# A decoder trunk on one core: the moving operands of the feed-forward products and the attention stage's regions laid at differing bytes modulo 64

## The chip, the core and the metric

The kernel runs on one core of one Trainium2 chip. The metric is device time in microseconds of that core, from the first to the last instruction of one launch with what lies around it. Lower is better. TensorE is called PE here, VectorE DVE, ScalarE ACT, GpSimd POOL and SyncE SP; PEld is the loading of PE's stationary operand, which the profile shows on a row of its own.

## What is computed

Two layers of a hybrid decoder over 512 tokens of 1024 channels, in float32, then a final norm:

```python
for l in range(2):
    h = rms_norm(x)                       # (512, 1024)
    proj = h @ w_in                       # 6656 columns: q, k, v, rotary q, k, v, gate g_r, merge gates
    y_a = stick_breaking(q, k, v) @ sb_w_out          # 8 heads of 64
    y_b = (group_norm(retention(q_r, k_r, v_r)) * silu(g_r)) @ ret_w_out   # 4 heads
    x = x + (g_a * y_a + g_b * y_b) @ w_o
    a, b = split(rms_norm(x) @ w_up)      # 2 * 2816 columns
    x = x + (silu(causal_conv3(a)) * b) @ w_down
return rms_norm(x)
```

## The kernel before

**Products in three passes.** Every large product is done with each float32 operand split into a high part (rounded to the format fp32r, which PE takes in one pass) and a low part (the rest). For one tile of 128 x 128 of the stationary operand and 256 or 512 columns of the moving operand, PE does three matmuls: high times high, high times low, low times high. `three` and `three_open` write them out. Each matmul loads its own stationary tile, so one weight load belongs to one matmul. ACT makes the high parts (copies into fp32r) and DVE the low parts (a subtraction).

**Who is moving and who is stationary.** In the projections from `w_in`, in the products with `sb_w_out`, `ret_w_out` and `w_o`, and in the first two pairs of up-projection tiles, the weight slab (`w_hi`, `w_lo`) is stationary and the token operand moves, 512 columns at a time: `u_hi`/`u_lo` (normed input), `osb` (attention output), `or_hi`/`or_lo` (retention output), `m_hi`/`m_lo` (merged branches). For the value columns it is the other way round: `u_hi`/`u_lo` stationary, the slab moving.

**Seven products.** The rest of the up-projection (9 rounds of two pairs a layer) is done by a Strassen-like scheme: the tokens and the channels are halved, seven combinations of the quarters are made once per layer (`comb_hi[k]`, `comb_lo[k]`, k = 0 to 6, each 4 tiles of 256 columns), and `product(n, k, ...)` multiplies combination k with a combination of the weight quarters. One product is 24 matmuls: 2 column tiles, 4 contraction tiles, 3 passes, each with `comb_hi[k]` or `comb_lo[k]` moving, 256 columns. Two layers of 9 rounds of 7 products are 3024 matmuls of 256 columns. The down-projection uses the same scheme with 7 products of 21 chunks in all: the gated activation is cut in chunks (`chunk_hi[n % 3]`, `chunk_lo[n % 3]`), of which the first two of three lie in `comb_hi[3]`, `comb_lo[3]` and `comb_hi[4]`, `comb_lo[4]` and the third in `chunk_hi2`, `chunk_lo2`. In layer 0 (`down_unit`) the chunk moves, 256 columns: 924 matmuls, of which 336, 336 and 252 read chunk 0, 1 and 2. In layer 1 (`token_unit`) the chunk is stationary and the weights move, 512 columns: 462 matmuls, 168, 168 and 126.

**Where the tiles lie.** SBUF tensors are placed by hand: `sb(name, shape, dt, where)` places a tile at byte `where` of each partition. The first tiles (`xs`, `u_hi`, `u_lo`, `w_hi`, `w_raw`, with `far_*` over them) come one after another. From `M` on lie the regions of the attention stage (`QK`, `VS`, `RQK`, `VR_`, `SG_`, `G_`, `TMP`), which the feed-forward stage uses anew: `g_raw`, `comb_hi[k]` at `s_hi_at[k]`, `comb_lo[k]` at `s_lo_at[k]`, and so on. All regions are whole multiples of 1024 bytes from `M`, and

```python
assert M % 64 == u_hi_at % 64 == w_hi_at % 64 == ring_at % 64
```

so that both operands of every large matmul start at the same byte modulo 64: byte 32. All but a few start at byte 32 modulo 128 too. The few lie behind the two buffers `ca` (8 * (S + 8) = 4160 bytes, which is 65 times 64): `comb_lo[5]`, `comb_hi[6]`, `comb_lo[6]`, `chunk_hi2` and `chunk_lo2` start at byte 96 modulo 128. A tile within an operand begins at a multiple of 512 bytes from the operand's start, so it keeps these remainders.

**Order.** Each engine has its own instruction list, written out by hand and tied by semaphores; PE's list is unrolled, 9106 matmuls.

Of the kernel before, what the change touches and what calls it, by code (L numbers as in the profile page):

```python
# [22 lines left out]
F32 = mybir.dt.float32  # L23
# [3 lines left out]
P = 128  # L27
S = 512
# [126 lines left out]
def trunk(nc, xt, wts, wdn, par, consts, rope, decay, last, out):  # L155
    with ExitStack() as ctx:
# [5 lines left out]
        def sb(name, shape, dt, where=None):  # L162
            n = 1
            for s in shape[1:]:
                n *= s
            size = n * {BF16: 2, mybir.dt.uint8: 1}.get(dt, 4)
            if where is None:
                where = at[0]
                at[0] += (size + 31) // 32 * 32
            return nc.alloc_sbuf_tensor_at(name, shape, dt, offset=where)  # L170

        K = 1024
        x_at = at[0] + 4 * KT
        xs = sb("xs", [P, KT + KT * S], F32)
        x = xs[:, KT:].rearrange("p (k s) -> p k s", k=KT)
        u_hi_at = at[0]
        u_hi = sb("u_hi", [P, KT, S], F32R)
        far_raw = sb("far_raw", [P, 4, SLAB], F32, u_hi_at)
        far_lo = sb("far_lo", [P, 4, SLAB], F32R, u_hi_at)
        u_lo_at = at[0]  # L180
# [20 lines left out]

        M = at[0] + 32
        assert M % 64 == u_hi_at % 64 == w_hi_at % 64 == ring_at % 64
        QK, VS, RQK, VR_, SG_, G_ = M, M + 16 * K, M + 32 * K, M + 48 * K, M + 64 * K, M + 80 * K
        TMP = M + 112 * K
        q2 = sb("q2", [P, SB_HEADS, S], F32R, QK)
        k2 = sb("k2", [P, SB_HEADS, S], F32R, G_)
        q_lo = [sb(f"q_lo{p}", [P, 2, S], F32R, (SG_ + 12 * K, TMP + 5 * K, G_ + 22 * K, G_ + 26 * K)[p])
                for p in range(SB_PAIRS)]
# [25 lines left out]

        att = sb("att", [P, ECOLS], F32, TMP)
        att_lo = sb("att_lo", [P, S], F32R, TMP)
        att_hi = sb("att_hi", [P, S], F32R, TMP + 2 * K)
        st_last = sb("st_last", [P, 256], F32R, TMP + 4 * K)
        beta = sb("beta", [P, ECOLS], F32, G_ + 16 * K)  # L240
        sp_hi = sb("sp_hi", [P, ECOLS], F32R, G_ + 16 * K)
        sp_lo = sb("sp_lo", [P, ECOLS], F32R, TMP)
        ynorm = sb("ynorm", [P, TT, 256], F32, TMP + 5 * K)
        g_raw = sb("g_raw", [P, FT, S], F32, M)
        first_raw = sb("first_raw", [P, 4, SLAB], F32, M + 28 * K)
        XYU = M + 88 * K + 8 * (S + 8) + 8 * K
        copy_x = sb("copy_x", [P, 2, S // 2], F32, XYU)
        copy_y = sb("copy_y", [P, 2, S // 2], F32, XYU + 2 * K)
        copy_u = sb("copy_u", [P, 2, S // 2], F32, XYU + 4 * K)
        late2 = sb("late2", [P, 4, S // 2], F32, XYU)  # L250
        PAST = XYU + 6 * K
        s_hi_at = [M + (44 + 8 * k) * K for k in range(6)] + [PAST + 4 * K]
        s_lo_at = [M + (48 + 8 * k) * K for k in range(5)] + [PAST, PAST + 8 * K]
        comb = [sb(f"comb{k}", [P, 4, S // 2], F32, s_lo_at[k]) for k in range(7)]
        comb_lo = [sb(f"comb_lo{k}", [P, 4, S // 2], F32R, s_lo_at[k]) for k in range(7)]
        comb_hi = [sb(f"comb_hi{k}", [P, 4, S // 2], F32R, s_hi_at[k]) for k in range(7)]
        t_raw = sb("t_raw", [P, PIECES, SLAB], F32, M + 44 * K)
        chunk_hi = [comb_hi[3], comb_hi[4], sb("chunk_hi2", [P, 4, S // 2], F32R, PAST)]
        chunk_lo = [comb_lo[3], comb_lo[4], sb("chunk_lo2", [P, 4, S // 2], F32R, XYU)]
        s_raw = [sb(f"s_raw{i}", [P, 4, S // 2], F32, M + at_k) for i, at_k in enumerate((84 * K, 88 * K, 92 * K + K // 2))]  # L260
        ca = sb("ca", [P, 2, S + 8], F32, M + 88 * K)
        cb_at = M + 88 * K + 8 * (S + 8)
        cb = sb("cb", [P, 2, S], F32, cb_at)
        cc = sb("cc", [P, 2, S], F32, cb_at + 4 * K)
        lastg = sb("lastg", [P, D], F32, cb_at + 4 * K)
# [1958 lines left out]
```

## Time and profile before

| | |
|---|---|
| median of 3 runs | 1582.34 us (1582.21 to 1583.85) |
| the profiled execution | 1581.26 us |
| its span, first to last instruction | 1579.5 us |
| PE busy | 1566.5 us, 99% |
| weight loads (PEld) busy | 1383.8 us, 88% |
| DVE busy | 1171.5 us, 74% |
| ACT busy | 769.3 us, 49% |
| POOL busy | 250.6 us, 16% |
| mean granted TensorE clock | 0.999 |

Matmuls are pipelined, and the length that the profile gives for one overlaps that of the next. What a matmul costs in a row of them is the distance from its start to the next one's start; it is called the pitch here. It is read from the timeline, as the time between two starts divided by the number of matmuls between them.

### The profile page before, as it was taken

To read this page: it belongs to the slowest core of one execution; us is meant where nothing else is said; L and a number is where in the kernel's file an instruction comes from. 1 tells how busy PE (TensorE), PEld (TensorE's weight loads), DVE (VectorE), ACT (ScalarE), POOL (GpSimd) and SP (SyncE) were. 2 spreads that over 40 slices of the span, in tenths; PEclk is the share of its full clock that TensorE was granted. 3 is DMA by queue.
4 is the path that set the end of the run, shared out by engine and by line. 5 is a ranking of instruction groups with operands and counts; after the bars stand their busy time and mean duration, and the time that the engine had idled before them with its cause. 6 is when DMAs were issued, how large, how long until landed. Compare 5 with 4: busy or idle time off the path is not lost. (4 is left out here: it accounts for less than half of the span.)

```text
span 1579.5 us, 22764 instructions
## 1 busy us (share of the span) xinstructions
PE 1566.5 (99%) x9106; PEld 1383.8 (88%) x9106; DVE 1171.5 (74%) x1295; ACT 769.3 (49%) x982; POOL 250.6 (16%) x270
## 2 busy tenths in 40 slices
PE   9999999999999999999999999999999999999998
PEld 7888888888888999999988888888888899999776
DVE  7257876786679877796972678658756898777877
ACT  5344334542355555664533533355332565556646
POOL 4000000000230222241240000000002212223310
PEclk9999999999999999999999999999999999999999
DMA  5332222222227888899223322222222388888991
GB/s 195 99 122 75 79 81 93 80 68 93 94 94 240 239 233 237 264 239 260 97 96 104 114 75 78 81 94 70 78 94 93 100 251 237 237 237 277 229 271 64
DMA packets 66628, 231.41 MB, mean 147 GB/s; under 512 B 7392, under 2 KB 7904, under 8 KB 66528
## 3 DMA queue, kind: packets, MB, share of 16 engines
q1 hardware_dynamic: 52272, 182.93, 33.4%
q0 software_dynamic: 12096, 41.95, 14.7%
q10 hardware_dynamic: 2160, 5.12, 1.1%
q8 instruction: 72, 1.18, 0.3%
q14 instruction: 28, 0.23, 0.0%
HBM read 225.78 MB, written 2.10 MB: 144 GB/s over the span
## 5 line engine op out<-in xcount | busy, mean ns | idle before, releaser
L1748 PE MATMUL ps<-u_hi,w_hi 128*128 128x512 f32 x768 | 301.3, 392 | 0.0
L1749 PE MATMUL ps<-u_lo,w_hi 128*128 128x512 f32 x768 | 299.3, 390 | 0.0
L1750 PE MATMUL ps<-u_hi,w_lo 128*128 128x512 f32 x768 | 299.1, 390 | 0.0
L1186 DVE TENSOR_TENSOR w_lo<-w_raw,w_hi 128x1024 fp32r<-128x1024 f32 x158 | 208.6, 1333 | 68.3 <-ACT w_hi L752 67.9
L752 ACT ACTIVATE w_hi<-w_raw 128x1024 fp32r<-128x1024 f32 x158 | 164.3, 1052 | 76.6 <-DMA w_raw<-wts 70.2
L1754 PE MATMUL ps<-comb_hi,far_hi 128*128 128x256 f32 x688 | 194.5, 283 | 0.0
L1755 PE MATMUL ps<-comb_lo,far_hi 128*128 128x256 f32 x688 | 194.1, 282 | 0.0
L1756 PE MATMUL ps<-comb_hi,far_lo 128*128 128x256 f32 x624 | 175.7, 282 | 0.0
L1750 PEld LDWEIGHTS ps<-u_hi,w_lo 128*128 128x128 f32 x768 | 144.2, 188 | 30.4
L1748 PEld LDWEIGHTS ps<-u_hi,w_hi 128*128 128x128 f32 x768 | 144.4, 188 | 28.4
L1749 PEld LDWEIGHTS ps<-u_lo,w_hi 128*128 128x128 f32 x768 | 144.4, 188 | 28.3
L1754 PE MATMUL ps<-comb_hi,w_hi 128*128 128x256 f32 x544 | 154.2, 283 | 0.4 <-DVE comb_lo L1415 0.3
L1756 PE MATMUL ps<-comb_hi,w_lo 128*128 128x256 f32 x544 | 153.8, 283 | 0.0
L1755 PE MATMUL ps<-comb_lo,w_hi 128*128 128x256 f32 x544 | 153.2, 282 | 0.0
L1754 PEld LDWEIGHTS ps<-comb_hi,far_hi 128*128 128x128 f32 x688 | 131.4, 191 | 0.8 <-issue 0.5
L1755 PEld LDWEIGHTS ps<-comb_lo,far_hi 128*128 128x128 f32 x688 | 131.5, 191 | 0.0
L1756 PEld LDWEIGHTS ps<-comb_hi,far_lo 128*128 128x128 f32 x624 | 118.8, 190 | 0.0
L1754 PEld LDWEIGHTS ps<-comb_hi,w_hi 128*128 128x128 f32 x544 | 103.5, 190 | 2.0 <-DVE w_lo L1349 0.6
L1756 PEld LDWEIGHTS ps<-comb_hi,w_lo 128*128 128x128 f32 x544 | 104.2, 192 | 0.0
L1755 PEld LDWEIGHTS ps<-comb_lo,w_hi 128*128 128x128 f32 x544 | 103.6, 190 | 0.0
L713 POOL TENSOR_TENSOR g_raw<-cc,cb 128x512 f32<-128x512 f32 x36 | 73.5, 2059 | 186.4 <-ACT cc L834 186.4
L1349 DVE TENSOR_TENSOR far_lo<-far_raw,far_hi 128x1024 fp32r<-128x1024 f32 x48 | 58.8, 1224 | 48.4 <-ACT far_hi L821 47.2
(325 smaller groups left out, 3402.6 us busy)
## 6 DMA issues: line engine op xcount, KB each, us to landing
w_raw<-wts SPq DMA_DIRECT2D x212, 512.0 KB, 3.5
far_raw<-wts SPq DMA_DIRECT2D x56, 512.0 KB, 3.6
t_raw<-wdn POOLq DMA_DIRECT2D x30, 512.0 KB, 9.8
w_raw<-wdn SPq DMA_DIRECT2D x24, 512.0 KB, 7.0
w_raw<-wts POOLq DMA_DIRECT2D x18, 512.0 KB, 10.3
far_raw<-wts POOLq DMA_DIRECT2D x16, 512.0 KB, 7.0
far_raw<-wdn SPq DMA_DIRECT2D x16, 512.0 KB, 8.3
t_raw<-wdn SPq DMA_DIRECT2D x10, 512.0 KB, 5.9
```

Of the source, the lines that this page charges most:

```text
L713: nc.gpsimd.tensor_tensor(g_raw[:, f, :], cc[:, h, :], cb[:, h, :], ALU.mult).then_inc(s_gf, 1)
L752: nc.scalar.activation(w_hi[:, s, :], w_raw[:, s, :], ACT.Copy).then_inc(s_hi, 1)
L1186: nc.vector.tensor_tensor(w_lo[:, s, :], w_raw[:, s, :], w_hi[:, s, :].bitcast(F32), ALU.subtract).then_inc(s_lo, 1)
L1349: nc.vector.tensor_tensor(part_lo(l, n, k), part_raw(l, n, k), part_hi(l, k).bitcast(F32), ALU.subtract).then_inc(s_elo, 1)
L1748: nc.tensor.matmul(dst, a_hi, b_hi, start=start, stop=False)
L1749: nc.tensor.matmul(dst, a_hi, b_lo, start=False, stop=False)
L1750: return nc.tensor.matmul(dst, a_lo, b_hi, start=False, stop=stop)
L1754: nc.tensor.matmul(dst, a_hi, b_hi, start=start, stop=False, skip_group_check=True)
L1755: nc.tensor.matmul(dst, a_hi, b_lo, start=False, stop=False, skip_group_check=True)
L1756: return nc.tensor.matmul(dst, a_lo, b_hi, start=False, stop=stop, skip_group_check=True)
```

## The change

No instruction is added, removed or moved, and none changes its shape: each engine has the same instructions in the same order, and only addresses differ. `sb` learns to place a tile at a byte that is no multiple of 32: it allocates a slightly wider tile at the multiple of 32 below and returns the part of it that begins at the wanted byte. Then

- the regions of the attention stage are displaced by 8 bytes (`QK`, `VS`), 16 bytes (`RQK`, `VR_`, `SG_`) and 48 bytes (`G_`), and `TMP` by 64;
- the moving operands of the seven products are displaced by `APART[k]` = 8, 16, 24, 40, 48, 56, 68 bytes, the high and the low part of one k alike;
- what lies behind them is pushed on by 64 bytes to make room, so that `chunk_hi2` and `chunk_lo2` come to byte 32 modulo 128.

The slabs and parts of the weights (`w_*`, `far_*`), `u_hi`, `u_lo`, `g_raw`, `t_raw` and `first_raw` stay where they were.

```diff
-            return nc.alloc_sbuf_tensor_at(name, shape, dt, offset=where)
+            if where % 32 == 0:
+                return nc.alloc_sbuf_tensor_at(name, shape, dt, offset=where)
+            apart = where % 32 // 4
+            tile = nc.alloc_sbuf_tensor_at(name, [shape[0], apart + n], dt, offset=where - 4 * apart)[:, apart:apart + n]
...
-        QK, VS, RQK, VR_, SG_, G_ = M, M + 16 * K, M + 32 * K, M + 48 * K, M + 64 * K, M + 80 * K
-        TMP = M + 112 * K
+        QK, VS, RQK, VR_, SG_, G_ = M + 8, M + 16 * K + 8, M + 32 * K + 16, M + 48 * K + 16, M + 64 * K + 16, M + 80 * K + 48
+        TMP = M + 112 * K + 64
...
-        XYU = M + 88 * K + 8 * (S + 8) + 8 * K
+        XYU = M + 88 * K + 8 * (S + 8) + 8 * K + 64
...
-        s_hi_at = [M + (44 + 8 * k) * K for k in range(6)] + [PAST + 4 * K]
-        s_lo_at = [M + (48 + 8 * k) * K for k in range(5)] + [PAST, PAST + 8 * K]
+        APART = (8, 16, 24, 40, 48, 56, 68)
+        s_hi_at = [M + (44 + 8 * k) * K + APART[k] for k in range(6)] + [PAST + 4 * K + 64 + APART[6]]
+        s_lo_at = [M + (48 + 8 * k) * K + APART[k] for k in range(5)] + [PAST + APART[5], PAST + 8 * K + 64 + APART[6]]
...
-        ca = sb("ca", [P, 2, S + 8], F32, M + 88 * K)
-        cb_at = M + 88 * K + 8 * (S + 8)
+        ca = sb("ca", [P, 2, S + 8], F32, M + 88 * K + 64)
+        cb_at = M + 88 * K + 8 * (S + 8) + 64
```

How far the two operands of a matmul lie apart modulo 128, before and after, with the number of matmuls:

| matmuls | columns | before | after |
|---|---|---|---|
| products 0 to 4 of the up-projection | 2160 of 256 | 0 | 8, 16, 24, 40, 48 |
| product 5 | 432 of 256 | 0 (high part), 64 (low) | 56 |
| product 6 | 432 of 256 | 64 | 4 |
| down-projection, layer 0, chunks 0 and 1 | 672 of 256 | 0 | 40, 48 |
| the same, chunk 2 | 252 of 256 | 64 | 0 |
| `osb`; `or`; `m` with weight slabs | 192; 384; 384 of 512 | 0 | 8; 16; 48 |
| down-projection, layer 1, chunks 0 and 1 | 336 of 512 | 0 | 88, 80 |
| the same, chunk 2 | 126 of 512 | 64 | 0 |
| `u_hi`, `u_lo` with weight slabs | 2904 of 512 | 0 | 0 |

The remaining matmuls, some 830, belong to the attention heads and the retention and are mostly narrower.

## Rows read from the trace of the kernel before

**Rows 1.** The page: span, busy time and, in 40 slices, the granted clock.

```profile
span 1579.5 us, 22764 instructions
PE 1566.5 (99%) x9106; PEld 1383.8 (88%) x9106; DVE 1171.5 (74%) x1295; ACT 769.3 (49%) x982; POOL 250.6 (16%) x270
...
PEclk9999999999999999999999999999999999999999
```

**Rows 2.** PE's waits: line, waited for: us in total, times, longest.

```profile
PE ps L2076 <- ACT xt_early L885: 2.9, 1, 2.9
PE ps L1754 <- DVE chunk_lo L1415: 2.2, 3, 1.2
```

**Rows 3.** Groups by shape: moving and stationary operand | busy us, mean ns | idle.

```profile
L1748 PE MATMUL ps<-u_hi,w_hi 128*128 128x512 f32 x768 | 301.3, 392 | 0.0
...
L1754 PE MATMUL ps<-comb_hi,far_hi 128*128 128x256 f32 x688 | 194.5, 283 | 0.0
...
L1748 PE MATMUL ps<-or_hi,w_hi 128*128 128x512 f32 x128 | 50.0, 390 | 0.0
L1748 PE MATMUL ps<-m_hi,w_hi 128*128 128x512 f32 x128 | 49.8, 389 | 0.0
```

**Rows 4.** Timeline of PE, products 2 and 3: start us; 49 rows, first and last.

```profile
581.65 0.28 PE L1754 MATMUL ps<-comb_hi,far_hi 128*128 128x256 f32 x1
...
587.41 0.28 PE L1754 MATMUL ps<-comb_hi,far_hi 128*128 128x256 f32 x1
```

**Rows 5.** Timeline of PE, products 5 and 6: 49 rows, first and last.

```profile
590.29 0.28 PE L1754 MATMUL ps<-comb_hi,far_hi 128*128 128x256 f32 x1
...
595.94 0.28 PE L1754 MATMUL ps<-comb_hi,w_hi 128*128 128x256 f32 x1
```

**Rows 6.** Timeline of PE, product 6 of the first round: 21 rows.

```profile
513.06 0.28 PE L1756 MATMUL ps<-comb_hi,far_lo 128*128 128x256 f32 x1
...
515.33 0.28 PE L1755 MATMUL ps<-comb_lo,w_hi 128*128 128x256 f32 x1
```

**Rows 7.** Timeline of PE, output projection, 512 columns: 25 rows.

```profile
430.17 0.39 PE L1748 MATMUL ps<-m_hi,w_hi 128*128 128x512 f32 x1
...
435.61 0.39 PE L1748 MATMUL ps<-m_hi,w_hi 128*128 128x512 f32 x1
```

**Rows 8.** Timeline of PE, token stage, chunk 2, 512 columns: 19 rows.

```profile
1492.21 0.40 PE L1754 MATMUL ps<-w_hi,chunk_hi 128*128 128x512 f32 x1
...
1496.40 0.39 PE L1754 MATMUL ps<-far_hi,comb_hi 128*128 128x512 f32 x1
```

**Rows 9.** Timeline of PE after the scores of one head.

```profile
125.21 0.40 PE L1748 MATMUL ps<-u_hi,w_hi 128*128 128x512 f32 x1
125.45 0.40 PE L1749 MATMUL ps<-u_lo,w_hi 128*128 128x512 f32 x1
125.68 0.39 PE L1750 MATMUL ps<-u_hi,w_lo 128*128 128x512 f32 x1
125.91 0.40 PE L1748 MATMUL ps<-u_hi,w_hi 128*128 128x512 f32 x1
...
126.38 0.39 PE L1750 MATMUL ps<-u_hi,w_lo 128*128 128x512 f32 x1
126.60 0.39 PE L1748 MATMUL ps<-u_hi,w_hi 128*128 128x512 f32 x1
```

**Rows 10.** VectorE's two convolution lines: duration ns min/median/max.

```profile
L1386 DVE SCALAR_TENSOR_TENSOR cc<-ca,pars,cc x44: 736/744/752, 477.4 to 1465.1; 128x512 f32<-128x512 f32 x44
...
L1389 DVE SCALAR_TENSOR_TENSOR cc<-ca,pars,cc x44: 750/752/754, 478.2 to 1465.9; 128x512 f32<-128x512 f32 x44
```

**Rows 11.** Stretches: busy us of PE, PEld, DVE, ACT, POOL; clock, DMA share.

```profile
600.00:640.00 40.00, 40.00 (x338) 40.00 (x337) 31.84 (x33) 23.31 (x30) 11.76 (x8) 1.00 0.83 235
680.00:720.00 40.00, 40.00 (x337) 40.00 (x337) 37.94 (x35) 20.92 (x23) 16.35 (x16) 1.00 1.05 228
```

**Rows 12.** The DMA that copies the queries: count, KB each, us to landing.

```profile
q<-q ACTq DMA_DIRECT2D x8, 256.0 KB, 3.7
```

More of the change, by code:

```diff
@@ L169, in sb @@
                 at[0] += (size + 31) // 32 * 32
-            return nc.alloc_sbuf_tensor_at(name, shape, dt, offset=where)
+            if where % 32 == 0:
+                return nc.alloc_sbuf_tensor_at(name, shape, dt, offset=where)
+            apart = where % 32 // 4
+            tile = nc.alloc_sbuf_tensor_at(name, [shape[0], apart + n], dt, offset=where - 4 * apart)[:, apart:apart + n]
+            if len(shape) == 2:
+                return tile
+            letters = "abcde"[:len(shape) - 1]
+            return tile.rearrange(f"p ({' '.join(letters)}) -> p {' '.join(letters)}", **dict(zip(letters[1:], shape[2:])))
         K = 1024
@@ L259, in trunk @@
         chunk_lo = [comb_lo[3], comb_lo[4], sb("chunk_lo2", [P, 4, S // 2], F32R, XYU)]
-        s_raw = [sb(f"s_raw{i}", [P, 4, S // 2], F32, M + at_k) for i, at_k in enumerate((84 * K, 88 * K, 92 * K + K // 2))]
-        ca = sb("ca", [P, 2, S + 8], F32, M + 88 * K)
-        cb_at = M + 88 * K + 8 * (S + 8)
+        s_raw = [sb(f"s_raw{i}", [P, 4, S // 2], F32, M + at_k) for i, at_k in enumerate((84 * K + 64, 88 * K + 64, 92 * K + K // 2 + 64))]
+        ca = sb("ca", [P, 2, S + 8], F32, M + 88 * K + 64)
+        cb_at = M + 88 * K + 8 * (S + 8) + 64
         cb = sb("cb", [P, 2, S], F32, cb_at)
```

## The prediction

> **What bounds the kernel now.** I read the page first: PE is busy for 1566.5 of 1579.5 us and its clock is at the full level, 2.4 GHz, in all 40 slices [rows 1]. Then what PE waits for: the longest entries are 2.9 and 2.2 us in all [rows 2]. So no transfer and no other engine sets the time; the sum of the distances between PE's matmuls does. The change touches no instruction, only the addresses that matmuls read. It can matter only through the pitch of a matmul, and the question is whether pitch depends on address.
>
> The grouped rows do not answer that, since their mean length overlaps the next matmul's: 283 ns for 256 columns, 389 to 392 ns for 512 [rows 3]. The timeline does. In products 2 and 3 of a late round, 48 matmuls of 256 columns start within 587.41 - 581.65 = 5.76 us: 120.0 ns each [rows 4]. The next two but one, products 5 and 6, take 595.94 - 590.29 = 5.65 us for 48: 117.7 ns each [rows 5]. Clock, shape and engine are the same. What differs is the place: `comb_lo[5]`, `comb_hi[6]` and `comb_lo[6]` lie 64 bytes off modulo 128 against the weights, while in products 2 and 3 both operands lie alike. Product 6 of the first round, entered after a wait and not from a running stream, does 20 matmuls in 515.33 - 513.06 = 2.27 us: 113.5 ns each [rows 6]. Streaming 256 columns at 2.4 GHz takes 106.7 ns, so the part over it is 13.3, 11.0 or 6.8 ns.
>
> With 512 columns the sign is the other way. Operands that lie alike: 24 in 435.61 - 430.17 = 5.44 us, 226.7 ns [rows 7], again 13.3 ns over the 213.3 ns of streaming. With chunk 2, 64 bytes off: 18 in 1496.40 - 1492.21 = 4.19 us, 232.8 ns [rows 8]. And even where operands lie alike the pitch has a memory: after a head's scores five matmuls take 126.38 - 125.21 = 1.17 us, 234 ns each, before the stream settles; the next one takes 0.22 us [rows 9]. So weight load and moving stream meet in some pattern that settles into a steady pitch, and the pattern knows the operands' relative place. The trace shows it at two relative places only, 0 and 64; the change moves to 4, 8, 16, 24, 40, 48, 56, 80 and 88, which no row shows.
>
> **A rule against the trace.** The Trainium skill, "SBUF — State Buffer", section "Who interferes with whom", gives PE two independent read ports, one for the moving operand and one for the weight load, and says that PE never waits on anyone. By that rule the relative place would not matter and the sum of this change would be nothing, 1582 us. The 120.0, 117.7 and 113.5 ns above, for one and the same shape, do not fit it, so the sum below goes by the rows.
>
> **The change, part by part.**
>
> *Products 0 to 4 and chunks 0 and 1 of layer 0's down-projection*: 2160 + 672 = 2832 matmuls of 256 columns leave the place where the pitch is 120.0 ns. Bounds: 113.5 ns [rows 6], which gives -6.5 ns each, -18.4 us; and 120.0 ns as now, nothing. Above 120.0 I know no steady row of this shape; for an upper bound I take the 6.1 ns by which the displaced 512-column row is dearer [rows 7, 8]: +17.3 us. I take 117.0 ns, near the 117.7 ns of the common displaced case with a little weight on 113.5: -3.0 x 2832 = -8.5 us.
>
> *Products 5 and 6*: 864 matmuls at 117.7 ns now. Bounds 113.5 (-3.6 us) and 120.0 (+2.0 us). At 117.0: -0.6 us.
>
> *Chunk 2 of layer 0's down-projection*: 252 matmuls come to lie alike, 117.7 to 120.0 ns: +0.6 us.
>
> *Output projection, retention output, attention output, and chunks 0 and 1 of layer 1*: 384 + 384 + 192 + 336 = 1296 matmuls of 512 columns leave the place where the pitch is 226.7 ns. Bounds: 232.8 ns [rows 8], +7.9 us; and, downwards, the same 6.5 ns that the 256-column rows have been seen to lose, -8.4 us. The nearest row is the one at 232.8, but it is one place out of many; I take half of its price, +3.05 ns: +4.0 us.
>
> *Chunk 2 of layer 1*: 126 matmuls from 232.8 to 226.7 ns, -0.8 us, and the irregular matmuls behind each of its seven stretches are fewer; -1.0 us together.
>
> *Attention and retention*: some 830 mostly narrower matmuls; at 3 ns either way 2.5 us, taken as nothing and kept for the range.
>
> *The unchanged 2904 matmuls of 512 columns* stay at 226.7 ns. Where they follow a displaced stretch they may need a few matmuls to settle, as in [rows 9], where five cost 5 x (234 - 226.7) = 37 ns. Some 40 such places would be 1.5 us, and most are there already; nothing.
>
> *DVE, ACT, POOL and the DMAs* get operands at bytes that are multiples of 4. Two convolution lines read `ca` one element past its start and at its start: 744 and 752 ns [rows 10]; a displaced read costs DVE nothing. The copy of the queries lands in 3.7 us [rows 12]; its target is now at another byte, and if it took twice as long, eight copies would cost at most 30 us in all, but PE has no wait for them among its longest [rows 2] and only a part of that could show. I put it at nothing. The engines behind PE have room in the rounds of seven products, DVE 31.84 and DMA 0.83 of 40 us [rows 11], so a 3% faster PE is still fed. In layer 0's down-projection DVE is busy for 37.94 us of 40 and the DMA share is 1.05, so there a gain much above 5% would turn into a wait for `chunk_lo`; at 2.5% it doesn't.
>
> Sum: -8.5 - 0.6 + 0.6 + 4.0 - 1.0 = -5.5 us. The profiled execution took 1581.26 us, 1.1 us under the median; so 1575.8 us on its scale and 1576.8 on the median's: **1577 us**.
>
> **The rivals.**
>
> *Strong gain (0.18).* The new places let the stream settle at 113.5 ns as in [rows 6]: 2832 x -6.5 = -18.4, 864 x -4.2 = -3.6, and the 512-column part between -4 and +4: 1556 to 1564, about 1560 us. For it: that pitch exists and is steady over 20 matmuls. Against it: in late rounds product 6 lies at the same place and does not reach it [rows 5].
>
> *Slower (0.34).* What decides is that lying exactly alike is the steady case, and each other place keeps the stream irregular. Then the 1296 wide matmuls go to 232.8 ns, +7.9 us, while the narrow ones stay at 120.0, and products 5 and 6 lose their 2.3 ns, +2.0; with +0.6 and -1.0 that is +9.5 us: 1592 us. It turns slower as soon as the wide loss, up to 7.9 us, outweighs the narrow gain: with the wide ones at 232.8 the narrow pitch must come under 117.4 ns to break even (products 5 and 6 included). The narrow pitch itself could rise, to 1600 and more. For it: [rows 8]; against it: [rows 5, 6], where displaced narrow matmuls are cheaper.
> Beside this rival stands a rule: the Trainium skill, "SBUF — State Buffer", section "Specifications (TRN2)", speaks of cachelines of 16 bytes and of a penalty for each crossing into a new one. An operand that starts 8 or 4 bytes into such a line touches one line more, in products 0, 2, 3, 5, 6 and `osb`, not in 1 and 4, `or` and `m`. No row of before has such an operand.
>
> *Nothing happens (0.19).* Only the 64-byte step counts, and smaller displacements are rounded away: products 0 to 4 stay at 120.0 ns, the wide ones at 226.7, and what is left, chunk 2 and products 5 and 6, is +0.6 - 1.0 + 2.0 = +1.6 us: 1584 us. For it: everything in the trace is in steps of 64; against it: nothing I can show.
>
> **How the numbers follow.** The forecast case, a small net gain, has 0.29, and ranges from 1568 to 1581. With the strong gain, the slower case and no effect, 0.18 + 0.34 + 0.19, that is all. The low end takes in the centre of the strong gain, 1560; the high end reaches past the slower case's 1592 to 1595. A measurement of this kernel tells 0.2%, 3.2 us, from no change. Faster by more than that: the strong gain and nearly all of the forecast case, 0.45. Within it: 0.21. Slower: 0.34.
>
> **What would show it.** In the timeline of the changed kernel: products 0 to 4 at about 117 ns a matmul instead of 120.0, and not all alike, since each k has its own displacement; `or`, `m` and `osb` at about 230 ns; `u` stretches at 226.7 as before; chunk 2 at 120.0 (256 columns) and 226.7 (512). PE's waits should stay under 15 us in all. The prediction is wrong if the products stay at 120.0 to the nanosecond (no effect of small steps), if any k stands above 120 (the slower case or worse), or if the wide matmuls drop below 226.7, which no row of before has.

## The result: slower by 0.4%

Before took 1582.98 us (1582.21 to 1583.85, 4 runs), the changed kernel 1588.32 us (1587.86 to 1590.89, 4 runs): a ratio of 1.0039, 95% interval 1.0027 to 1.0052. The forecast was 1577 us, faster, with a range from 1560 to 1595; the time lies on the other side of no change, within the range.

The page of the kernel after, with the lines that answer to [rows 1]:

```profile
span 1586.9 us, 22764 instructions
...
PE 1574.0 (99%) x9106; PEld 1384.2 (87%) x9106; DVE 1171.6 (74%) x1295; ACT 769.6 (48%) x982; POOL 250.4 (16%) x270
...
PEclk9999999999999999999999999999999999999999
```

PE is still busy for 99% of the span, at the full clock in all 40 slices, so the 7.4 us more of this span (1586.9 - 1579.5) are PE's own. PE's waits (line, waited for: us in total, times, longest), for [rows 2]:

```profile
PE ps L1762 <- DVE chunk_lo L1423: 2.9, 3, 1.4
...
PE ps L2084 <- ACT xt_early L893: 1.1, 1, 1.1
PE ps L1762 <- DVE cb L1379: 1.0, 1, 1.0
```

With the new one, for `cb`, they come to 5.0 us, against 5.1 in [rows 2]: no longer than before. The groups by shape, for [rows 3]:

```profile
L1756 PE MATMUL ps<-or_hi,w_hi 128*128 128x512 f32 x128 | 50.6, 395 | 0.0
...
L1756 PE MATMUL ps<-m_hi,w_hi 128*128 128x512 f32 x128 | 50.4, 394 | 0.0
```

The mean of the displaced wide matmuls rose from 389 or 390 ns to 394 or 395. That mean overlaps with the next matmul, so what a matmul costs has to be read from the starts. The timeline of PE after, a few starts (in us, then the modelled length):

```profile
364.54 0.47 PE L1756 MATMUL ps<-or_hi,w_hi 128*128 128x512 f32 x1
...
409.10 0.39 PE L1756 MATMUL ps<-m_hi,w_hi 128*128 128x512 f32 x1
...
453.26 0.39 PE L1756 MATMUL ps<-u_hi,w_hi 128*128 128x512 f32 x1
...
581.67 0.28 PE L1762 MATMUL ps<-comb_hi,w_hi 128*128 128x256 f32 x1
...
584.47 0.28 PE L1762 MATMUL ps<-comb_hi,far_hi 128*128 128x256 f32 x1
...
587.35 0.28 PE L1762 MATMUL ps<-comb_hi,far_hi 128*128 128x256 f32 x1
...
595.93 0.28 PE L1762 MATMUL ps<-comb_hi,w_hi 128*128 128x256 f32 x1
...
598.87 0.28 PE L1762 MATMUL ps<-comb_hi,w_hi 128*128 128x256 f32 x1
...
1194.26 0.40 PE L1756 MATMUL ps<-m_hi,w_hi 128*128 128x512 f32 x1
...
1239.06 0.39 PE L1756 MATMUL ps<-u_hi,w_hi 128*128 128x512 f32 x1
```

From 364.54 to 409.10 lie the 192 matmuls of `or` in layer 0 (16 bytes further from their weights than before): 232.1 ns each. From 409.10 to 453.26 lie the 192 of `m` (48 bytes): 230.0 ns; from 1194.26 to 1239.06 those of `m` in layer 1, at the same addresses: 233.3 ns. So one place can have more than one steady pitch. Before, `or` took 227.2 ns read in the same way and `m` the 226.7 ns of [rows 7]. Product 1 (16 bytes) is the 24 matmuls from 581.67 to 584.47, 116.7 ns; product 2 (24 bytes) follows to 587.35, 120.0 ns; product 6 (4 bytes, 595.93 to 598.87) takes 122.5 ns, where [rows 5] had 117.7. So some narrow products gained, some did not, one lost, and every wide one lost.

Read that way over all rounds (means of the distances of a product, first round and waits left out), the pitch stands so:

| product | 0 | 1 | 2 | 3 | 4 | 5 | 6 |
|---|---|---|---|---|---|---|---|
| before, ns | 119.4 | 120.0 | 120.0 | 120.0 | 120.0 | 118.0 | 117.6 |
| after: distance of its high tile | 8 | 16 | 24 | 40 | 48 | 56 | 4 |
| after, ns | 118.0 | 116.6 | 120.1 | 119.6 | 118.3 | 119.2 | 122.5 |

### The profile page after: what moved, and what is told of

Read it like the earlier page. It is cut to its first block, busy times and chain, and to the rows that moved or that the text cites. A ratio compares the mean times of both kernels' runs of the same rounds, so it can differ in the third digit from the quotient of the medians.

```text
span 1586.9 us, 22764 instructions
## 1 busy us (share of the span) xinstructions
PE 1574.0 (99%) x9106; PEld 1384.2 (87%) x9106; DVE 1171.6 (74%) x1295; ACT 769.6 (48%) x982; POOL 250.4 (16%) x270
## 3 DMA queue, kind: packets, MB, share of 16 engines
q10 hardware_dynamic: 2160, 5.12, 1.1%
## 4 chain that ended last, share of the span: by engine, by line
PE 96%; DMA 3%; DVE 0%; issue 0%; ACT 0%; POOL 0%; DVEq 0%; POOLq 0%; ACTq 0%
PE ps L1756 19%; PE ps L1758 19%; PE ps L1757 18%; PE ps L1762 12%; PE ps L1764 12%; PE ps L1763 12%; DMA far_raw<-wdn 1%; PE ps L1885 1%; PE ps L1874 1%; DMA w_raw<-wdn 1%; PE ps L1852 1%; PE ps L1856 1%; PE ps L2009 0%; PE ps L1896 0%; PE ps L1822 0%
## 5 line engine op out<-in xcount | busy, mean ns | idle before, releaser
L1764 PEld LDWEIGHTS ps<-comb_hi,far_lo 128*128 128x128 f32 x624 | 117.8, 189 | 0.0
```

What stands on the lines that cost most here:

```text
L1764: return nc.tensor.matmul(dst, a_lo, b_hi, start=False, stop=stop, skip_group_check=True)
```

## The experiments

"Distance" is the place of the token operand less the place of the weight operand, modulo 128 bytes unless another number is named. Ratios are to the kernel before, run on the same chip alongside; they are the ones on record, and differ by up to 0.05% from the quotient of the two medians. The pitches, waits and stage times of a kernel come from one profiled execution. The first four kernels ran together (before: 1581.47 us, 29 runs).

**e1_regions: only the attention regions are displaced.** The regions and `TMP` lie as in the change; the products' tiles and what lies behind them are back where they were before. In part:

```diff
-        APART = (8, 16, 24, 40, 48, 56, 68)
+        APART = (0, 0, 0, 0, 0, 0, 0)
```

> The kernel before, with only the attention stage's regions displaced as in the change (8, 8, 16, 16, 16, 48 bytes); the products' tiles stay. Theory P (the pitch of a matmul follows from the relative place of its two operands, matmul by matmul, so the parts of the change add up): the 960 matmuls of 512 columns that move osb, or and m go from about 227 to about 232 ns, 960 x 5 ns = +4.8 us, the rest unchanged: about +5 us, ratio 1.003. Rival Q (the loss comes from the products that are off the 16-byte grid, and the wide matmuls matter only through them): under +1 us.

It took 1587.02 us (5 executions), ratio 1.0040 (1.0027 to 1.0053): the whole loss. Theory P, with 1.003, holds; rival Q does not. Its timeline of PE around `m` in layer 0:

```profile
408.51 0.40 PE L1756 MATMUL ps<-m_hi,w_hi 128*128 128x512 f32 x1
...
453.31 0.39 PE L1756 MATMUL ps<-u_hi,w_hi 128*128 128x512 f32 x1
```

192 matmuls in 44.80 us are 233.3 ns each, against 226.7 before. All `or`, `m` and `osb` of both layers came to 231.6, 233.3 and 232.7 ns; here `m` was at 233.3 in both layers.

**e2_products: only the tiles of the seven products are displaced.** The edit is the other half, with `APART` kept:

```diff
-        QK, VS, RQK, VR_, SG_, G_ = M + 8, M + 16 * K + 8, M + 32 * K + 16, M + 48 * K + 16, M + 64 * K + 16, M + 80 * K + 48
+        QK, VS, RQK, VR_, SG_, G_ = M, M + 16 * K, M + 32 * K, M + 48 * K, M + 64 * K, M + 80 * K
```

> The kernel before, with only the tiles of the seven products displaced (8, 16, 24, 40, 48, 56, 68) and what lies behind them pushed on; the attention regions stay. Theory P, from the changed kernel's pitches by product (118.0, 116.6, 120.1, 119.6, 118.3, 119.2, 122.5 ns against 119.4, 120, 120, 120, 120, 118.0, 117.6) and +6.5 ns for 336 wide matmuls of layer 1's down-projection: -0.6 -1.5 +0.1 -0.3 -1.3 +0.5 +2.1 +0.3 +2.2 = about +1.5 us, ratio 1.001. Rival Q: nearly all of the change's +5.3 us.

1581.5 us, ratio 0.9997 (0.9988 to 1.0006), without a twelfth execution that took 5547.74 us: no difference, where theory P had 1.001. Each product showed the pitch of the table above. The narrow matmuls earned nothing that can be measured (the 1.7 us that the wide ones of layer 1's down-projection lose are in this time as well). The two halves, +0.40% and -0.03%, add up to the change's +0.39% as well as such intervals can tell.

**e4_base32: every tile 32 bytes further.** Operands keep their relative places, and all bytes modulo 64 change from 32 to 0:

```diff
-        at = [(nc.sbuf_base + 31) // 32 * 32]
+        at = [(nc.sbuf_base + 31) // 32 * 32 + 32]
```

> The kernel before, with every tile pushed on by 32 bytes: all operands keep their relative places, but start at byte 0 modulo 64 instead of 32. Theory P (the relative place): within 0.1% of before, pitches 120.0, 117.7 and 226.7 ns to the nanosecond. Rival S (the absolute place: a start inside a block of 64 bytes costs part of a block more): the 13.3 ns over streaming shrink, by up to 6.7 ns each for some 8000 matmuls, tens of us faster.

1581.47 us, ratio 0.9998 (0.9989 to 1.0007). Its products 1 to 4 ran at 120.0 ns, product 6 at 117.6 and `m` at 226.7, each as before. A common step of 32 bytes changes nothing, so rival S is out; what counts is where the two operands lie against each other.

**e3_all16: the best distance for all products, 0 for the wide ones.** All seven products and layer 0's chunks at 16 bytes, regions and layer 1's chunks at 0; the chunks get tiles of their own in each layer. In part:

```diff
-        APART = (8, 16, 24, 40, 48, 56, 68)
+        APART = (16, 16, 16, 16, 16, 16, 16)
...
-        chunk_hi = [comb_hi[3], comb_hi[4], sb("chunk_hi2", [P, 4, S // 2], F32R, PAST)]
+        CHUNK = (16, 0)
+        chunk_hi = [[sb(f"chunk_hi{l}_{c}", [P, 4, S // 2], F32R, w + CHUNK[l]) for c, w in enumerate((M + 68 * K, M + 76 * K, PAST))]
+                    for l in range(DEPTH)]
...
```

> The kernel before, with all seven products' moving operands displaced by 16 bytes, and layer 0's chunks too; layer 1's chunks (stationary there) stay at 0, and so do the attention regions. Theory P: every one of them at the 116.6 ns that product 1 has at 16 bytes: 2160 x -3.4 - 432 x 1.4 - 432 x 1.0 - 672 x 3.4 - 252 x 1.1 = about -11 us, ratio 0.993. Rival R (product 1 is cheap because of the product ahead of it, not because of its 16 bytes): the products settle near 120 and the time is within 2 us of before.

1579.72 us, ratio 0.9988 (0.9978 to 0.9998): 1.8 us instead of 11. One round of its timeline, products 0 to 4:

```profile
598.66 0.28 PE L1765 MATMUL ps<-comb_hi,w_hi 128*128 128x256 f32 x1
...
609.54 0.28 PE L1765 MATMUL ps<-comb_hi,far_hi 128*128 128x256 f32 x1
```

These are 96 matmuls in 10.88 us, 113.3 ns each, the lowest pitch seen; in most rounds it was 116.7, in a few 118.7, and in one round 120.0. So the step on which I had counted, a lower pitch, was there, and the gain still was not. The sum of all the distances between narrow matmuls that are under 135 ns fell from 467.1 to 457.8 us (3916 and 3909 of 3948). What stood against it were PE's waits:

```profile
PE ps L1765 <- DVE chunk_lo L1426: 4.3, 4, 1.7
PE ps L2087 <- ACT xt_early L896: 2.6, 1, 2.6
PE ps L1765 <- DVE cb L1382: 1.9, 4, 0.7
PE ps L1765 <- DVE w_lo L1415: 1.7, 1, 1.7
```

chunk_lo and xt_early went from 5.1 us to 6.9, and two new ones, for `cb` and `w_lo`, add 3.6. Summed over the whole feed-forward stages, what the distances hold beyond a regular pitch rose from 9.9 to 16.9 us. By their means (119.3 and 117.1 ns) the pace gained 8.6 us; less 7.0 us that leaves 1.6, beside the 1.0 by which the two spans differ.

The next three ran together (before: 1583.2 us, 23 runs).

**e7_down0: all products at 16, both down-projections at 0.** It asks whether PE's pace counts in the down-projection of layer 0.

```diff
-        CHUNK = (16, 0)
+        CHUNK = (0, 0)
```

> As the kernel with all at 16 bytes, but the first layer's down-projection reads its chunks at distance 0 again, so that some 910 matmuls go back from 117 to 120 ns, 2.5 to 3 us of TensorE's own work more. Theory W (the end of the first layer's down-projection is bound by the tiles that VectorE and the DMA queues make ready, so that a faster TensorE only waits longer): the time is that of the kernel with all at 16 within 0.05%, ratio to before 0.999, and the waits of more than 1 us near 732, 746 and 751 us shrink by the 2.5 to 3 us. Rival R (TensorE's pace binds there): 3 us slower than the kernel with all at 16, ratio to before 1.001.

1579.21 us, ratio 0.9977 (0.9967 to 0.9987). Its stretches (busy us and count of PE, PEld, DVE, ACT, POOL; clock, DMA share, GB/s), then PE's waits within them, first for e3_all16:

```profile
725.00:765.00 40.00, 35.66 (x296) 34.77 (x295) 31.00 (x29) 19.81 (x22) 3.50 (x4) 1.00 0.73 205
...
PE ps L1765 <- DVE chunk_lo L1426: 2.6, 3, 1.7
PE ps L1765 <- DVE w_lo L1415: 1.7, 1, 1.7
```

and for e7_down0:

```profile
725.00:765.00 40.00, 38.89 (x326) 38.72 (x325) 35.32 (x33) 23.54 (x27) 3.49 (x4) 1.00 0.74 213
...
PE ps L1765 <- DVE chunk_lo L1426: 1.1, 1, 1.1
```

With the faster pitch PE was busy for only 35.66 of the 40 us and issued 296 matmuls in them; with the slower one 326. The 924 matmuls of that projection went from 117.2 to 119.5 ns, 2.1 us more, and still layer 0's products and down-projection together took 291.0 us instead of 293.5. In these two profiles PE's faster pace in this stage is worth nothing, as theory W has it. By how much the stage comes out shorter they do not tell: the down-projection of layer 0 took 113.8 us in e3_all16 and 111.8 here, but 113.4 when this same program ran again (e9_repeat), and 112.3 with the faster pitch in e6_all16b. The total was forecast to stay at e3_all16's 0.9988; the two intervals overlap.

**e6_all16b: products 5 and 6 at 16 modulo 256 too.** As e3_all16, and:

```diff
-        s_lo_at = [M + (48 + 8 * k) * K + APART[k] for k in range(5)] + [PAST + APART[5], PAST + 8 * K + APART[6]]
+        s_lo_at = [M + (48 + 8 * k) * K + LOW[k] for k in range(5)] + [PAST + LOW[5], PAST + 8 * K + LOW[6]]
```

with `LOW[5]`, `LOW[6]` and `APART[6]` at 144.

> As the kernel with all at 16 bytes, but products 5 and 6 lie 16 bytes from their weights modulo 256 and not only modulo 128. Theory P256 (the pattern repeats with 256 bytes or more): both fall from 117.8 and 118.6 ns to 116.7, 864 matmuls in 1.3 us less. Rival P128 (it repeats with 128): they stay. In the time, if TensorE's own pace still binds in the rounds, 1 us less than the kernel with all at 16, ratio to before 0.998; if the waits for the copies of product 6 take the gain up, 0.999 as there.

1578.68 us, ratio 0.9980 (0.9966 to 0.9994). Neither theory's numbers came out, since the common level had changed. Product 4 was at 118.7 ns in 15 of 18 rounds, at 116.7 in two and at 113.3 in one, at the same addresses as in e3_all16, where it was at 116.7 in 13 rounds. Products 5 and 6 fell in with it: where the round stood at 118.7 they did too, and in the two rounds at 116.7 product 5 was at 116.7 and 116.8. In e3_all16, at 16 modulo 128 but with its low tile at 144 modulo 256, product 5 stood at 117.8 beside neighbours at 116.7. So 16 and 144 modulo 256 are different places, and distances modulo 128 do not say it all. Its products 1 to 3 in a round, 72 matmuls in 8.54 us (118.6 ns):

```profile
540.68 0.28 PE L1766 MATMUL ps<-comb_hi,w_hi 128*128 128x256 f32 x1
...
549.22 0.28 PE L1766 MATMUL ps<-comb_hi,far_hi 128*128 128x256 f32 x1
```

**e5_scan: other distances.** Products 0 to 6 at 4, 12, 20, 32, 36, 64 and 96 bytes (the low tile of 5 at 192 and both of 6 at 224 modulo 256), `osb` and `or` at 32, `m` at 64.

```diff
-        APART = (8, 16, 24, 40, 48, 56, 68)
+        APART = (4, 12, 20, 32, 36, 64, 96)
```

> A map rather than a bet on the time. The operands of the products lie 4, 12, 20, 32, 36 and 64 (192 for its low tile) bytes from those of the weights, product 6 at 224 modulo 256; osb and or at 32, m at 64. Theory P (only the distance 0 lets 512 columns run at 226.7 ns; every other distance costs them 2% to 3%): or, osb and m all come out at 231 to 234 ns, the four stages of or and m together 3 to 5 us longer than before, and the time 2 to 6 us above the kernel before. Rival G (the pattern repeats with 64 bytes or 32): m at 64 stays at 226.7 ns, and with 32 or and osb too, so that the time is within 0.1% of before or lower by what the products gain. For the products, if a displacement of 4 inside 16 bytes is what made product 6 slow (122.5 ns), products 0, 2 and 4 (4, 20 and 36) are at 121 to 123 ns; if it was something of that place alone, they are at 116 to 120.

1590.99 us, ratio 1.0046 (1.0029 to 1.0063). Its timeline: `m` between the first two starts, then products 5, 6, 0, 1 and 2 in turn:

```profile
409.68 0.39 PE L1756 MATMUL ps<-m_hi,w_hi 128*128 128x512 f32 x1
...
453.63 0.39 PE L1756 MATMUL ps<-u_hi,w_hi 128*128 128x512 f32 x1
...
593.97 0.28 PE L1762 MATMUL ps<-comb_hi,far_hi 128*128 128x256 f32 x1
...
596.80 0.28 PE L1762 MATMUL ps<-comb_hi,w_hi 128*128 128x256 f32 x1
...
599.64 0.28 PE L1762 MATMUL ps<-comb_hi,w_hi 128*128 128x256 f32 x1
...
602.60 0.28 PE L1762 MATMUL ps<-comb_hi,w_hi 128*128 128x256 f32 x1
...
605.42 0.28 PE L1762 MATMUL ps<-comb_hi,far_hi 128*128 128x256 f32 x1
...
608.35 0.28 PE L1762 MATMUL ps<-comb_hi,far_hi 128*128 128x256 f32 x1
```

`m` at distance 64: 228.9 ns, between 226.7 and 233, and `or` at 32: 233.8. So 0 is the cheapest wide place found, and 64 is not the same as 0: rival G is out, and theory P missed `m`, which it had at 231 to 234, and the time, which it had at most 6 us above before. Of the narrow ones, 24 matmuls each, 4 bytes (599.64 to 602.60) cost 123.3 and 20 bytes 122.1 ns; over all rounds 4, 20 and 36 bytes cost 123.0, 122.0 and 121.0 ns, and 12, 32, 64 and 96 bytes 117.7, 116.7, 117.8 and 118.4. Product 6's 122.5 in the changed kernel was no accident of its place: a distance of 4, or of 4 beyond a multiple of 16, cost 121 to 123 ns wherever it was tried.

The next two ran together (before: 1582.39 us, 22 runs).

**e8_all32: all products at 32, down-projections at 0.** As e7_down0 with `APART = (32,) * 7`.

> All seven products 32 bytes from their weights (products 5 and 6 with 160 modulo 256), the chunks of both down-projections and the attention's regions at 0. In the scan 32 gave 116.7 ns in every round where its neighbours lay elsewhere. Theory D (the distance alone sets the pitch): products 0 to 4 at 116.7 in all 18 rounds, none at 113.3 or 118.7, and the time that of the kernel with 16 bytes and the chunks at 0, ratio to before 0.998. Rival H (where neighbouring products lie alike, the pitch also depends on how they fell into step, and is handed on from product to product): rounds with levels below and above 116.7, as with all at 16, and a time anywhere from 0.996 to 1.000.

1578.81 us, ratio 0.9979 (0.9965 to 0.9992). Products 1 to 4 were at 116.5 to 116.9 ns in 17 of 18 rounds and at 117.8 in one. At 32 bytes theory D holds nearly, where 16 bytes had several levels. Products 5 and 6, at 160 modulo 256 in three of their four tiles, stood between 117.2 and 118.9.

**e9_repeat: the program of e7_down0 once more, on another chip.**

> The same program as the one with all products at 16 bytes and both down-projections at 0, in a new execution on another chip. Theory D (the pitch is a property of the addresses): the rounds at 113.3 and 118.7 ns stand at the same places as in its first profile. Rival H (it depends on how the streams fell into step in that execution): other rounds at 113.3 and 118.7. The ratio to before should be 0.998 again, 0.997 to 0.999; at 1.000 or above it would not have been a gain.

1578.23 us, ratio 0.9976 (0.9965 to 0.9986). In e7_down0 the second round of layer 1 ran products 2 to 4 at 113.3 ns, 72 matmuls between these two starts:

```profile
1303.36 0.28 PE L1765 MATMUL ps<-comb_hi,far_hi 128*128 128x256 f32 x1
...
1311.52 0.28 PE L1765 MATMUL ps<-comb_hi,far_hi 128*128 128x256 f32 x1
```

and here the same 72 took 8.40 us, 116.7 ns:

```profile
1302.78 0.28 PE L1765 MATMUL ps<-comb_hi,far_hi 128*128 128x256 f32 x1
...
1311.18 0.28 PE L1765 MATMUL ps<-comb_hi,far_hi 128*128 128x256 f32 x1
```

Rival H holds: at 16 bytes the same addresses give 113.3, 116.7 or 118.7 ns in different rounds and executions, and a product hands its level on to the next one. What picks the level, no run shows. The profile of this run, the slowest of its 12 executions (1583.55 us), also showed a loss late in layer 1. PE's two longest waits:

```profile
PE ps L2087 <- ACT xt_early L896: 4.8, 1, 4.8
...
PE ps L2087 <- ACT ca L851: 1.3, 1, 1.3
```

and three stretches from 1470 to 1482 us, columns as above:

```profile
1470.00:1474.00 4.00, 0.22 (x1) 0.22 (x2) 4.00 (x5) 1.81 (x3) 0.41 (x1) 0.77 0.43 138
1474.00:1478.00 4.00, 4.00 (x12) 3.32 (x12) 3.79 (x4) 3.01 (x4) 1.33 (x2) 0.50 0.70 106
1478.00:1482.00 4.00, 4.00 (x21) 3.23 (x21) 1.77 (x3) 2.09 (x5) 0.86 (x1) 0.88 1.06 196
```

In the first down-projection units of layer 1 PE has to turn rows of `x`, and waits for ACT and DVE to empty the banks. Here it stood for 1.3 us and a little later for 4.8 us, its clock fell to the lower level, 1.2 GHz (0.50), and after the wait it did 12 matmuls in 4 us. The kernel before, same place:

```profile
1474.00:1478.00 4.00, 3.75 (x21) 3.15 (x22) 3.79 (x4) 3.01 (x5) 1.74 (x2) 1.00 0.74 147
1478.00:1482.00 4.00, 4.00 (x22) 3.30 (x21) 3.80 (x4) 3.50 (x5) 1.24 (x2) 1.00 1.03 211
```

There the wait was 2.9 us, the clock stayed at 1.00, and the same 8 us from 1474 held 43 matmuls and not 33. The Trainium skill, "TensorE: Matmul & The Clock Gate", section "What's actually happening", says that an idle TensorE is put back to 1.2 GHz; the trace agrees, with its 0.50. Looking back, e2_products had this as well (wait 4.2 us, mean clock 0.83 from 1465 to 1485, last stage 125.2 us for before's 120.1). Its layer 1 products had taken 181.4 us, for 181.6 before, so a long wait does not need a gain there.

**e10_layer0 and e11_layer1: one layer each.** The last two (before: 1581.38 us, 23 runs) give the products of one layer 16 bytes and those of the other 0:

```diff
...
-        comb_hi = [sb(f"comb_hi{k}", [P, 4, S // 2], F32R, s_hi_at[k]) for k in range(7)]
+        comb_hi = [[sb(f"comb_hi{l}_{k}", [P, 4, S // 2], F32R, s_hi_at[k] + APART[l]) for k in range(7)] for l in range(DEPTH)]
```

with `APART = (16, 0)` and `(0, 16)`, and `comb`, `comb_lo` in the same way.

> Of the kernel with all products at 16 bytes and both down-projections at 0, only layer 0's products stay at 16; layer 1's go back to 0. Theory C (PE's pace sets the time only up to a point: early arrival at the transposes in layer 1's down-projection is paid with a wait, and where that wait is long the clock drops to half for some microseconds, 2 to 6 us in all): layer 0's seven products and down-projection 2 to 3 us shorter than before (about 291.5 us for 294.0), layer 1's products as before (181.5), the wait for xt_early 1 to 3 us, the granted clock between 1465 and 1485 us at 1.00, the last stage 120 to 121 us, and the time 2.5 us below before, ratio 0.9984, as good as with both layers displaced. Rival A (the gains of the two layers simply add, the clock's fall was chance): half the gain of 0.9977, so ratio 0.9988 to 0.9990, and the last stage no shorter than there.

> The other half: only layer 1's products at 16 bytes, layer 0 as before. Theory C: layer 1's products 2 to 3 us shorter (about 179 us for 181.6), but the wait for xt_early is over 3.5 us, the granted clock between 1465 and 1485 us under 0.95 and the last stage 2 to 6 us longer than before's 120.1; the time is within 0.1% of before, ratio 0.9995 to 1.001. Rival A: the last stage takes 120 to 121 us and the ratio is 0.9985.

Their times don't decide: 1580.67 us, ratio 0.9999 (0.9983 to 1.0015), and 1580.27 us, 0.9990 (0.9977 to 1.0003). Theory C had 0.9984 for the first and 0.9995 or more for the second, and rival A 0.9988 to 0.9990 and 0.9985; the two intervals take in both theories. Single executions went from 1577.2 to 1589.0 us with the same program, and the two profiles are of extreme ones, the fastest of e10_layer0 and the slowest of e11_layer1. Their stages go as theory C says. The stretch from 1465 to 1485 us of e10_layer0, and its wait:

```profile
1465.00:1485.00 20.00, 18.66 (x95) 15.10 (x93) 17.65 (x16) 12.32 (x17) 6.13 (x7) 1.00 1.05 264
...
PE ps L2087 <- ACT xt_early L896: 1.3, 1, 1.3
```

and of e11_layer1:

```profile
1465.00:1485.00 20.00, 15.15 (x66) 12.26 (x65) 17.04 (x15) 12.24 (x17) 6.44 (x5) 0.83 0.88 190
...
PE ps L2087 <- ACT xt_early L896: 4.8, 1, 4.8
```

By stages (us, from the starts in the trace):

| | layer 0: products and down-projection | layer 1: products | wait for `xt_early` | clock, 1465 to 1485 | layer 1: down-projection to the end |
|---|---|---|---|---|---|
| before | 294.0 | 181.6 | 2.9 | 1.00 | 120.1 |
| after | 293.9 | 183.2 | 1.1 | 1.00 | 120.6 |
| e1_regions | 294.5 | 181.4 | 1.5 | 1.00 | 119.6 |
| e2_products | 292.9 | 181.4 | 4.2 | 0.83 | 125.2 |
| e3_all16 | 293.5 | 180.1 | 2.6 | 1.00 | 120.6 |
| e4_base32 | 295.0 | 182.1 | 1.5 | 1.00 | 119.0 |
| e5_scan | 296.6 | 182.1 | 1.3 | 1.00 | 121.7 |
| e6_all16b | 293.4 | 180.8 | 2.0 | 0.91 | 120.9 |
| e7_down0 | 291.0 | 178.6 | 3.8 | 0.91 | 122.2 |
| e8_all32 | 291.6 | 180.0 | 4.5 | 0.91 | 123.8 |
| e9_repeat | 292.1 | 179.5 | 4.8 | 0.83 | 126.3 |
| e10_layer0 | 291.2 | 181.6 | 1.3 | 1.00 | 118.6 |
| e11_layer1 | 294.3 | 180.2 | 4.8 | 0.83 | 125.5 |

In the profiles with the longer waits, 3.8 to 4.8 us, the clock fell and the last stage took 122 to 126 us; in those with 1.1 to 2.9 us it held, but for e6_all16b. e7_down0 and e9_repeat are the same program, and differ by 1 us in each of the first two columns and by 4 in the last.

That a gain in layer 1, or PE's early arrival, causes the longer wait is not shown: e8_all32 and e10_layer0 came to the first of these transposes at 1462.5 and 1462.2 us and then waited 4.5 and 1.3 us. How often the clock falls can be read from the mean clock, which is on record for every execution; in the profiles of e2, e8, e9 and e11, with the longest waits, it is 0.997 or 0.998. It is that low in 10 of 97 executions of the kernel before (median 1586.4 us, against 1581.8 for the other 87) and in 16 of 82 of the seven kernels with products at 16 or 32 bytes and the wide operands left alone (1583.3 against 1578.8). So the kernel before most likely pays this too, though no trace of it shows the fall; a difference between 10 in 97 and 16 in 82 can be chance.

## Why the prediction was wrong

Its steps in order, with the sums over the profiled executions.

1. *The time is the sum of PE's distances, and the pitch depends on the relative place.* Right for this change. e4_base32 shows that it is the relative place. The rule that the prediction took from the Trainium skill ("SBUF — State Buffer", "Who interferes with whom"), two ports and a PE that never waits, does not give these pitches. Why the two streams settle at them, no run shows.
2. *Products 0 to 4 and the chunks at 117.0 ns: -8.5 us with products 5 and 6 and chunk 2 of layer 0.* This step failed. I took one common displaced pitch from the one displaced place that the trace showed, 64 bytes. The new places have pitches of their own, 116.6 to 122.5 ns. All narrow distances under 135 ns sum to 466.2 us (3914) against 467.1 (3916): a mean of 119.1 ns for 119.3, and -0.6 us instead of -8.5. The bound of 120.0 for products 5 and 6 was passed by product 6, and chunk 2 came to 118.6 ns, not to 120.0.
3. *1296 wide matmuls at half the price of [rows 8]: +4.0 us.* The mechanism was right and the size too small; 4.9 to 5.0 of the 6.1 ns were due, not half of them. `or` and `m` cost 231.7 ns in the mean, `osb` 232.5, and the wide matmuls of the last stage went from 229.4 to 233.0. That is 384 x 4.9 + 384 x 5.0 + 192 x 5.0 = 4.8 us, and 461 x 3.6 = 1.7 us for the last stage: +6.4 us, in which chunk 2 is counted.
4. *Chunk 2 of layer 1: -1.0 us.* It did not come: 232.5 ns after 233.4. The prediction had both operands lie alike here. They do modulo 128, but `PAST` and `XYU` lie 4160 + 64 = 4224 bytes and whole kilobytes from `M`, which is 128 modulo 256, and `M` and the weights are alike modulo 256. That this is another place than 0 is shown by the kernels with chunks 0 and 1 at 0. In e7_down0, product 2 of the last stage has 24 matmuls of chunk 1, 18 of chunk 2 and then 24 of the next chunk 0 between these starts:

```profile
1499.96 0.39 PE L1765 MATMUL ps<-far_hi,chunk_hi 128*128 128x512 f32 x1
...
1505.40 0.41 PE L1765 MATMUL ps<-w_hi,chunk_hi 128*128 128x512 f32 x1
...
1509.59 0.39 PE L1765 MATMUL ps<-w_hi,chunk_hi 128*128 128x512 f32 x1
...
1515.04 0.39 PE L1765 MATMUL ps<-far_hi,chunk_hi 128*128 128x512 f32 x1
```

That is 226.7, 232.8 and 227.1 ns. With 256 columns, in layer 0 of the same kernel, chunks 0 and 1 at 0 cost 119.7 and 120.0 ns and chunk 2 cost 118.7.
5. *DVE, ACT and the DMAs at nothing.* Right for this change: beyond the regular pitch the feed-forward stages held 10.7 us, for 9.9 before. The sentence that a pace 2.5% faster brings no wait for `chunk_lo` would not have held: in e3_all16, at a pitch 1.8% lower, that wait was 4.3 us for 2.2.

-0.6 + 6.4 + 0.8 = +6.6 us, of the 7.4 between the two spans; 0.7 of the rest lies in the first stage (336.6 for 335.9 us), where nothing large moved and which took 335.9 to 338.1 us in the experiments without a cause in the addresses. The medians differ by 5.3 us.

The rival that happened is *slower*: the wide matmuls at 232.8 ns and the narrow ones at 120.0, forecast 1592 us. It gave +9.5 us; the narrow matmuls, -0.6 us where it had +2.6, took some of that back. *Nothing happens* fell with e1_regions, since displacements of 8, 16 and 48 bytes are no less dear than 64. *Strong gain* is refuted as a forecast, though its 113.3 ns exist. The penalty for crossing 16-byte lines ("SBUF — State Buffer", "Specifications (TRN2)", in the Trainium skill) fits in part: 4, 20, 36 and the 4 of product 6 are the dear ones, but 12 bytes, which crosses as well, is among the cheap ones at 117.7 ns, 8, 24, 40 and 56, which cross too, cost 118.0 to 120.1, about as much as 0 or less, and the wide matmuls pay for 16, 32 and 48, which do not cross. As the weights stayed at multiples of 16 in all kernels, the runs do not tell the distance from the place in the line for these odd steps.

The version that beats both kernels has the wide operands at distance 0 and the seven products at 16 or 32: 0.9976 to 0.9979 in three runs of 11 or 12 executions each, 1578 to 1579 us, 0.2% under before. Its pitch alone would give 6.6 us in e7_down0 (3948 matmuls, 119.3 to 117.6 ns); about 3.6 us of them came. In its profile 2.4 us went into distances beyond the regular pitch (12.3 us for 9.9), the waits among them, and the first stage was 1.9 us longer, without a cause in the addresses. The clock's fall is no large part of it: none of its 12 executions has a mean clock under 0.999.

## What to carry to other kernels

When PE is busy for 99% of the span, its start-to-start distances are the time. Measure them for each pair of operands and each width before placing tiles: a distance that helps 256 columns can cost 512 columns 2 to 3%, and one displaced place says little about the next. Try displacements one shape at a time; here two halves of one edit had a price of +0.4% and of nothing, while the same idea with the wide operands left alone gave -0.2%. And before counting a faster pitch as time, look where PE will then wait. Two places that look alike modulo 128 need not be alike: compare them modulo 256 as well.

## What was not expected of the hardware

- At 2.4 GHz one 256-column matmul with its own weight load took 113.3, 116.7, 117.7, 118.7, 120.0 or 122 to 123 ns, steady over whole products, by the relative place of the two operands; one of 512 columns 226.7 at distance 0, 228.9 at 64 and 230.0 to 234 at 8, 16, 32 and 48.
- A distance of 128 modulo 256 is not a distance of 0: chunk 2 cost 232.8 ns between stretches at 227 (512 columns), and 118.7 beside 120.0 (256 columns), in e7_down0.
- At distance 16, neighbours alike, one program showed 113.3, 116.7 and 118.7 ns in different rounds, other rounds in another execution, and the level is handed on from product to product. At 32 it stayed at 116.7 in 17 of 18 rounds. `m` at 48 had two levels as well, 230.0 and 233.3 ns.
- Moving everything by 32 bytes changes none of it.
- After the waits of 3.8 to 4.8 us at the transposes of layer 1, and once after one of 2.0 us, PE ran at 1.2 GHz for a while (from 1474 to 1478 us in e9_repeat).
